# A routing stage reordered: the shared expert's first product split around the count, router products a tile later, last loads swapped

## The reference

```python
def moe_ffn(h, router_w, router_bias, w_gate, w_up, w_down, sh_gate, sh_up, sh_down):
    scores = jax.nn.sigmoid(h @ router_w)                       # T x 64
    _, idx = lax.top_k(scores + router_bias, TOP_K)             # 8 of 64 experts
    s_sel = jnp.take_along_axis(scores, idx, axis=-1)
    gates = s_sel / jnp.sum(s_sel, axis=-1, keepdims=True) * ROUTED_SCALE
    ...                                                         # tokens sorted by expert
    def expert_block(args):
        tok, e = args
        xb = h_pad[tok]
        hid = jax.nn.silu(xb @ w_gate[e]) * (xb @ w_up[e])      # 1024 -> 256
        return hid @ w_down[e]                                  # 256 -> 1024
    ...
    routed = jax.ops.segment_sum(y, buf_tok, num_segments=t + 1)[:t]
    shared = (jax.nn.silu(h @ sh_gate) * (h @ sh_up)) @ sh_down
    return routed + shared
```

## Time and profile before

| | us |
|---|---|
| timed runs: median (lowest, highest) | 1887.0 (1885.19, 1892.93) |
| the profiled execution, its own time | 1887.84 |
| its span, first to last instruction | 1886.0 |
| PE busy | 1663.1 (88%) |
| DVE busy | 571.2 (30%) |
| ACT busy | 310.5 (16%) |
| POOL busy | 208.5 (11%) |
| mean DMA rate | 297 GB/s, 560.88 MB |

### The profile page before, as it was taken

The page is one execution under the profiler, slowest core; times in us unless marked ns, Lnnn a source line. Parts: engine busy times, 40 slices in busy tenths (PEclk is TensorE's granted clock), DMA queues, the critical chain, the costliest instruction groups (busy, mean ns, idle before and its releaser), DMA issues. The chain is left out here.

```text
span 1886.0 us, 23152 instructions
## 1 busy us (share of the span) xinstructions
PE 1663.1 (88%) x8531; PEld 742.8 (39%) x8531; DVE 571.2 (30%) x1351; ACT 310.5 (16%) x684; POOL 208.5 (11%) x197
## 2 busy tenths in 40 slices
PE   5999998889999999999995599888789899979896
PEld 2544444454434343334432244454333333333232
DVE  2032675355222122222210551474421111111112
ACT  2002442130111111111110111171100101000001
POOL 0300342001111111111110000030000000000000
PEclk9999999999999999999998799898899999999998
DMA  9414992026999999999994924002699999999993
GB/s 353 145 66 148 378 357 97 1 108 277 417 391 413 419 415 403 408 406 401 416 413 185 411 90 151 32 1 79 262 418 400 420 419 402 418 420 414 418 397 128
DMA packets 125505, 560.88 MB, mean 297 GB/s; under 512 B 17426, under 2 KB 22945, under 8 KB 75216
## 3 DMA queue, kind: packets, MB, share of 16 engines
q1 hardware_dynamic: 106960, 512.28, 67.9%
q0 software_dynamic: 17248, 43.62, 6.1%
q10 hardware_dynamic: 1184, 3.47, 0.5%
HBM read 550.02 MB, written 26.80 MB: 306 GB/s over the span
## 5 line engine op out<-in xcount | busy, mean ns | idle before, releaser
L1686 PE MATMUL ps<-wb,pool 128*32 128x512 f32 (+2 forms) x2608 | 488.1, 599 | 21.6 <-issue 21.5
L1686 PEld LDWEIGHTS ps<-wb,pool 128*32 128x32 f32 (+2 forms) x2608 | 160.6, 124 | 309.2 <-issue 309.2
L1700 DVE TENSOR_TENSOR ffn_hid<-ffn_sg,ps 128x256 f32<-128x256 f32 x71 | 29.9, 421 | 611.4 <-ACT ffn_sg L1694 611.4
L1730 PE MATMUL ps<-pool,ffn_hidT 128*32 128x512 f32 (+2 forms) x584 | 166.2, 606 | 23.8 <-DVE ffn_hidT L1715 10.8
L1730 PE MATMUL ps<-hT,ffn_hidT 128*32 128x512 f32 (+2 forms) x680 | 158.0, 599 | 19.5 <-DVE ffn_hidT L1715 14.6
L1593 POOL DMA_INDIRECT pool<-h_rows,ffn_index x71 | 75.6, 1065 | 651.9 <-DVE ffn_index L1643 324.3
L2324 PE MATMUL ps<-wb,hT 128*128 128x512 f32 x320 | 141.1, 602 | 1.6 <-issue 1.6
L1694 ACT ACTIVATE ffn_sg<-ps 128x256 f32<-128x256 f32 x71 | 27.2, 383 | 492.2 <-PE ps L1686 492.2
L1730 PE MATMUL ps<-sh_wd,ffn_hidT 128*32 128x512 f32 (+2 forms) x272 | 100.3, 597 | 4.7 <-DVE ffn_hidT L1715 2.7
L1748 PE MATMUL ps<-x_res,rw 128*128 128x512 f32 x224 | 103.1, 603 | 0.9 <-ACT x_res L1776 0.9
L1656 PEld LDWEIGHTS ps<-const,pool 128*128 128x128 f32 x568 | 77.5, 194 | 66.5 <-issue 63.2
(11 more groups left out here) (299 smaller groups left out, 1770.9 us busy)
## 6 DMA issues: line engine op xcount, KB each, us to landing
wb<-in_expert_w_gate_dram SPq DMA_DIRECT2D x108, 1024.0 KB, 13.1
wb<-in_expert_w_up_dram SPq DMA_DIRECT2D x108, 1024.0 KB, 18.5
pool<-in_expert_w_down_dram SPq DMA_DIRECT2D x52, 1024.0 KB, 19.3
hT<-in_expert_w_down_dram SPq DMA_DIRECT2D x52, 1024.0 KB, 17.2
wb<-in_ada_w_dram SPq DMA_DIRECT2D x24, 2048.0 KB, 11.8
sh_wd<-in_expert_w_down_dram SPq DMA_DIRECT2D x24, 1024.0 KB, 20.0
mix_yr<-y_rows SPq DMA_DIRECT2D x8, 2048.0 KB, 11.9
wb<-in_diff_w_in_dram SPq DMA_DIRECT2D x6, 2048.0 KB, 16.8
```

Source lines behind the costliest of these rows:

```text
L1686: mm = nc.tensor.matmul(core.ps[lo:lo + width, gu_bank(n), :], xT[:, n % 2, k, lo:lo + width], w[:, k], start=k == 0, stop=k == KD - 1, sk ...
L1700: nc.vector.tensor_tensor(hid[:, n % 2, :], sg[:, n % 2, :], core.ps[:, gu_bank(n), F:2 * F], ALU.mult).then_inc(hid_ready, 1)
L1730: mm = nc.tensor.matmul(core.ps[lo:lo + width, down_bank(half), :], hidT[:, n % 2, k, lo:lo + width], wd_at(q % DR, half, k), start=k == 0 ...
```

## The change

In `project_out`, the router product of tile i - 1 takes the place of that of tile i, the fold of the loop goes behind it, and DVE's copies follow suit:

```diff
@@ project_out, PE @@
                         if i < len(streams) - 1:
                             spread_ffn(i)
                         if i >= 1:
-                            fold(i - 1)
-                        pair_of(i)
+                            pair_of(i - 1)
+                for i in range(max(NT - 4, 0), NT - 3):
+                    fold(i)
+                if NT > 2:
+                    pair_of(NT - 3)
                 spread_ffn(len(streams) - 1)
                 if NT > 2:
                     fold(NT - 3)
@@ project_out, DVE @@
-                    if half == 0 and n >= 4:
-                        take_pair(n // 2 - 2)
+                    if half == 0 and n >= 6:
+                        take_pair(n // 2 - 3)
+                if NT > 2:
+                    take_pair(NT - 3)
                 norm.dve_rows(dve, NT - 1)
```

In `feed_forward`, tile 0's shared gate/up product is cut into three parts: ahead of the count, behind the transposes of the gates, and behind the products that spread them. ACT's silu and DVE's product of tile 0 move behind; DVE's constant casts move from the front to behind the ids:

```diff
-        def pe_shared_gate_up(pe, i):
+        def pe_shared_gate_up(pe, i, lo=0, hi=KD):
             if i >= 2:
                 pe.wait_ge(sh_hid, i - 1)
-            for k in range(KD):
+            for k in range(lo, hi):
                 mm = nc.tensor.matmul(core.ps[:, i % 2, :], h(k, i), ...)
-            mm.then_inc(sh_gu, 1)
+            if hi == KD:
+                mm.then_inc(sh_gu, 1)
@@ PE @@
                 pe.wait_ge(wgu_in, 32)
-                pe_shared_gate_up(pe, 0)
+                part = 5 if NT > 2 else 3
+                pe_shared_gate_up(pe, 0, 0, part)
                 pe.wait_ge(mask_ready, 1)
...
                 mm.then_inc(vg_turned, 1)
+                pe_shared_gate_up(pe, 0, part, part + 1)
                 pe.wait_ge(pm_ready, 1)
...
                     if i % 2 == 1:
                         mm.then_inc(g_ready, 1)
+                pe_shared_gate_up(pe, 0, part + 1)
                 for n, (i, half) in enumerate(back):
@@ ACT @@
-                act_shared_silu(act, 0)
                 act.wait_ge(vg_turned, 1)
...
                                    core.ps[:, g_bank(2 * b), 0:2 * U]).then_inc(g_taken, 1)
+                act_shared_silu(act, 0)
                 for n, (i, half) in enumerate(back):
@@ DVE @@
-                link(nc.vector.memset(own_slots[:], 0.0))
-                ...                                        # unit marks, casts of tok_hi and tok_lo
-                link(ins)
                 link(nc.vector.tensor_scalar(score[:], score[:], 1.0, None, ALU.add))
...
                 nc.vector.tensor_copy(r.eid[:], core.ps[0:1, 7, 384:384 + E]).then_inc(eid_ready, 1)
-                dve_shared_hidden(dve, 0)
+                link(nc.vector.memset(own_slots[:], 0.0))
+                ...                                        # the same marks and casts
+                link(ins)
                 dve.wait_ge(v_ready, 1)
...
+                dve_shared_hidden(dve, 0)
                 dve_shared_hidden(dve, 1)
```

SP's loop issues gate/up of the last expert ahead of the last two downs; ACT gets an activation on a scratch tile, with the root's function, behind the last round of layer 1 and at the start of the combination:

```diff
@@ feed_forward, SP @@
                     sp_gate_up(sp, q)
-                    sp_down(sp, q - LAG)
-                for q in range(E - LAG, E):
+                    if q - LAG < E - 2:
+                        sp_down(sp, q - LAG)
+                for q in range(E - 2, E):
                     sp_down(sp, q)
@@ feed_forward, ACT, behind the rounds @@
                 if not last:
                     act_y(act, R - 1)
+                else:
+                    nc.scalar.activation(table_of[:], core.c("ident")[:, 0:1], ACT.Sqrt)
                 further(act, over, None, lambda b, e, n: fb_act(act, b, e, n))
```

And in the combination the first tile's second half is read as three rows and one row, and added row by row:

```diff
@@ combine_project, SP @@
                 rows(0)
-                rows(1)
+                sp.dma_start(yr[:, 1, 0:HALF - 1], y_view[0][:, HALF:TOP_K - 1, :]).then_inc(y_in[1], 16)
+                sp.dma_start(yr[:, 1, HALF - 1], y_view[0][:, TOP_K - 1, :]).then_inc(y_last, 16)
@@ combine_project, DVE @@
+                        if (t, half) == (0, 1):
+                            for j in range(HALF - 1):
+                                link(nc.vector.tensor_tensor(acc, acc, v[:, j], ALU.add))
+                            dve.wait_ge(y_last, 16)
+                            nc.vector.tensor_tensor(acc, acc, v[:, HALF - 1], ALU.add).then_inc(y_used, 1)
+                            dve.wait_ge(y_used, 2)
+                            continue
                         link(nc.vector.tensor_tensor(v[:, 0:2], v[:, 0:2], v[:, 2:4], ALU.add))
```

More of the change, by code:

```diff
@@ L1439, in feed_forward @@
             norm = RowNorm(core, st, tiles)
+            table_of = st.sb("table_of", [P, 1])
             back_ready, summed, x_ready, gain_in, done, stored = (
@@ L2065, in _ @@
                 nc.vector.tensor_copy(r.eid[:], core.ps[0:1, 7, 384:384 + E]).then_inc(eid_ready, 1)
-                dve_shared_hidden(dve, 0)
+                link(nc.vector.memset(own_slots[:], 0.0))
+                for s in range(UNITS):
+                    nc.vector.memset(mine[s * UNIT:(s + 1) * UNIT, s, :], 1.0)
+                for i in range(NT):
+                    nc.vector.tensor_copy(info[:, i, :, 16], core.c("tok_hi")[:, i:i + 1].to_broadcast([P, R]))
+                    ins = nc.vector.tensor_copy(info[:, i, :, 17], core.c("tok_lo").to_broadcast([P, R]))
+                link(ins)
                 dve.wait_ge(v_ready, 1)
@@ L2256, in combine_project @@
         ss, rs = st.sb("ss", [P, TILES]), st.sb("rs", [P, 3, TILES])
-        y_in = [st.sem("y_in0"), st.sem("y_in1")]
+        y_in, y_last = [st.sem("y_in0"), st.sem("y_in1")], st.sem("y_last")
+        table_of = st.sb("table_of", [P, 1])
         y_used, x_ready, own = st.sem("y_used"), st.sem("x_ready"), st.sem("own")
```

## The result

The changed kernel took 1870.07 us (median of 4 runs, 1868.22 to 1870.70) where the kernel before took 1886.26 on the same chip (4 runs): ratio 0.9905, 95% interval [0.9884, 0.9927]. On another chip it took 1868.52 beside 1886.05, ratio 0.9907 [0.9889, 0.9925]. The forecast was 1871.0. Its profiled execution took 1868.22 us (span 1866.3), the one of before 1887.84.

The account below looks back on a forecast made before the run. TensorE was taken to bound layer 0's rounds, the weight stream layer 1. Terms 5.6 - 0.1 + 4.3 + 4.2 + 1.0 + 1.3 + 0 = 16.3 us took 1887.84 to 1871.5, set at 1871.0 for the median; range 1865 to 1879.

Parts of the forecast that it names:

- Router products: Layer 0's projection: router products one tile later remove two TensorE waits; 5.6 us gained, bounds 4.3 to 6.1.
- Rival (d): Projection's tail takes its wait back, TensorE standing for the pair copies: 1.5 of 5.6 left, 1875.1 us; chance 0.07.
- Layer 0's split: Layer 0's routing: split gains 0.5 us, clock costs 0.7, earlier weights worth nothing; value -0.1, bounds -2 to +1.5.
- Layer 1's split: Layer 1's routing: earlier count lets first weights issue 4.3 us sooner and the rest follows; value 4.3, bounds 0.7 and 5.6.
- Rival (c): Layer 1's head start given back through half clock in the eight remaining pieces; about 1 us left, 1874.3; chance 0.14.
- Last weights: Layer 0's last round: gate/up 63 ahead of down 62 shortens TensorE's stop; value 4.2 us, bounds 0 and 4.5.
- The second term: Layer 0's last round: without TensorE's stop the clock would not fall, so 1.7 us more goes.
- Rival (b): End of layer 0 gains nothing: gate/up 63 lands when it did and the clock falls; 1875.2 us; chance 0.10.
- Rival (e): Slower: split leaves TensorE in short bursts and the clock stays at 1.2 GHz; 1926 us if throughout; chance 0.04.
- Eighth row and tables: Combination stage: eighth row earlier gains 1.0 us, root table prefetch 1.3; the same prefetch at the program's end 0.
- rival (a): The last table load, at the program's end, goes too; 1869.7 us; chance 0.17.
- The signs: Wrong if layer 1's count wait exceeds 2 us, its stream shows early gaps, or half clock exceeds 12 us in either routing.

Follow-up runs that it names:

- f3: The changed kernel with layer 0's first expert weights held back until the fifth turn of the rows; 1869.38 us, ratio 0.9912 to the kernel before.
- f2: The changed kernel with layer 1's first expert weights held back until the third turn of the rows; 1873.07 us, ratio 0.9927 to the kernel before.
- g4: The same kernel as f4, run on a third chip; 1871.04 us, ratio 0.9918 to the kernel before.
- f4: The changed kernel with layer 1's count behind two of six pieces instead of three and the last table prefetch behind the branch; 1871.09 us, ratio 0.9920.
- e4: The changed kernel with down 62 ahead of gate/up 63 again in layer 0; ratio 0.9947 to the kernel before.
- g1: The kernel before, unedited, run again for a second trace; 1888.24 us, ratio 0.9999 to its twin.
- g2: The changed kernel with layer 0's combination as before: eighth row with its half, no root table prefetch there; ratio 0.9929 to the kernel before.
- g3: The changed kernel with only the last root table prefetch moved behind the branch of the further rounds; 1870.34 us, ratio 0.9907 to the kernel before.
- e1: The changed kernel with the router products back in their old order in the projection; ratio 0.9938 to the kernel before.
- e3: The changed kernel with layer 1's shared product unsplit, in one piece ahead of the count; ratio 0.9937 to the kernel before.

## Why the prediction was right, point by point

**Router products.** Right, 5.8 to 6.0 us for 5.6: both waits went, and what came back behind the loop lay in the last tiles' waits even more than assumed (PE's waits there, 0.73 us for DVE and 0.81 us for ACT, became none and 0.55). Rival (d) is out: the waits at the tail are 0.55 and 1.52 us, no longer than they were.

**Layer 0's split.** Right: 0.5 to 0.8 us at equal clock, 0.5 forecast. The stage grew by 0.35 us, since 5.7 us of lower clock lay in it instead of 3.3. That the charge for the clock came true is partly luck: the unsplit order had 3.3, 6.8 and 2.8 us of it in three traces, the split one 3.3 to 6.2. That the earlier weights are worth nothing there f3 shows by the opposite edit.

**Layer 1's split.** Right in mechanism: the first weights came 4.4 us earlier in the first pair of traces and 4.1 in the second, 4.3 forecast, and f2 shows that the end follows them nearly one to one (4.8 us of delay, 4.2 at the last round). The size holds for the clock that the traces had; at full clock it is some 3.0 us, because DVE's own chain then sets the start, 7.8 us behind the first piece. What I had not worked out is how near the bound behind it was, too. Rival (c), the head start given back, needs round 0 about 0.9 us later than it came. g4 is such a case, with one more piece moved and 10 us more of lower clock; f4, the same kernel with less of it, was past the bound by 0.3 us only, so the clock and not the piece made most of it. Neither of the changed kernel's two traces came to the bound.

**Last weights.** The stop of 2.8 us went, as said, and the stage to the last round became 2.1 us shorter (2.9 against the second trace of before; the term was 2.5). The second term failed: "PE's stop was what preceded the fall of the clock ... so 1.7 us more goes". The 1.7 us were in the difference of the first two traces, but e4 and g1 keep the stop and run the round at full clock, so they are not the change's. It was a stretch that happened to fall there, and the argument from a shorter stop elsewhere was from a single execution. Rival (b) is out: by order alone the weights came in time. Rival (e) is out too: PEclk was 0.95 over layer 0's routing stage, beside 0.97 before.

**Eighth row and tables.** The stage gained 2.3 us (1.9 to 2.0 by g1 and g2) for 2.3 forecast. In the first pair of traces the last addition's end, counted from the rows' read, came 1.21 us earlier (0.8 to 0.9 against g1 and g2), and the rest of the stage took 1.1 less, for the load of 1.28: DVE's small operation on the sum of squares now stands open for 0.2 us that the load used to cover. By the 2.66 us per switch of the Trainium skill ("ScalarE: Activation LUTs", What ACT_TABLE_LOAD costs) the stage would have gained 3.7, an estimate from the page's figure (1.0 + 2.66); the measurement decides. At the end of the program the load stayed, as said, so rival (a) is out, and g3 shows that its place was the reason: moved behind the branch, the prefetch takes out 1.0 us. The trace agrees with the Trainium skill's statement that loads are placed per block ("ScalarE activation tables: per-element evaluation and per-set limits", Table sets in the compiler and the runtime): even the square, which had no load ahead of it before, got one when it became the first function behind the branch.

**What the sum left out.** The first pair of traces differs by 19.6 us, not 16.3. Of the surplus, 1.8 us lie in layer 1's attention (266.45 against 264.66), where nothing was edited: the trace of before has 5.2 us more of lower clock there (34.3 for 29.1), the second one does not (29.0). Another 1.9 us lie between layer 1's first weights and its last round. These repeat in g1 (514.50), so they are hardly chance; the table of rounds shows them arising after round 8, 1.2 of them by round 17. No single part brings them back (512.4 to 513.3 in e1 to e4 and g2). What makes them stays open. The medians are 16.2 and 17.5 us apart. They lie below the traces' difference, since both profiled executions of before were above its median (by 1.6 and 3.2 us) and those of after below theirs (by 1.9 and 0.2). So the forecast of 1871.0 was also helped a little: a clock term that was not the change's, against a gain that was not in the sum. Its own working gives 1870.7, not 1871.0 (1887.0 less 16.3), and -0.2 for layer 0's split, not -0.1; neither matters here.

**The signs.** One of the signs of being wrong came up and meant nothing: the stretch from layer 1's first piece to round 0 had 16.0 us at 1.2 GHz, more than the 12 us named, but before the change it had 16.2. The sign should have been set against the kernel before.

## What to carry to other kernels

Before crediting a move, find out what starts the stage's bound: where a stream of weights sets the end, an earlier first issue is worth nearly its whole lead up to the slack of the other path (work that slack out too), and where the rounds on TensorE do, it is worth nothing. A table prefetch holds only along straight code; put it behind the last branch before its use. A stretch of lower clock seen once in one trace belongs to that execution until a second trace has it in the same place. Taking half of such a stretch off a stage is right only while TensorE is what the stage waits for; look for the wait of the other engine first.

## What the runs showed that I had not expected

The stretches of lower clock differ between executions of the same program: the same wait of 3.12 us was followed by full clock in the first trace of before (and in e1) and by 6.8 us of half clock in g1 (2.8 us of time). The first pieces of layer 1's shared product, behind the same wait of 0.61 us, ran with 5.4 to 6.2 us of it in most traces, with 8.8 (g4), with 2.8 (f3, f4), or with none (e3, e1). They move a stage by up to 3 us, so two traces a few us apart say little on a single edit unless each stage is put to one clock.

The program's time up to the first projection scatters by 3.6 us over the fourteen traces (310.8 to 314.4) while, from there on, two pairs of traces of one kernel agree within 0.4 us (1572.1 and 1572.5; 1552.5 and 1552.3). The third pair does not: f4 and g4 took 1549.8 and 1552.9 us, by the lower clock. Counting each stage from a fixed instruction resolved parts of 1 us that the medians of 4 to 12 runs did not.
